# A sigmoid gate computed by its own table function, and another order of the last instructions of a decoder layer

## The chip, the cores and the metric

The kernel runs on one core of a Trainium2 chip. The metric is device time in microseconds (us), the median of several runs. The engines are named as the profile names them: PE (TensorE: matmuls; PEld are its weight loads), DVE (VectorE), ACT (ScalarE), POOL (GpSimd), SP (SyncE, which here only issues DMAs).

## The reference, cut to what matters

One layer of a decoder trunk on x of shape (1, 1024, 2048): an input projection feeds two groups of gated recurrences, their readouts go through an output projection, and then comes the stage that this change is about:

```python
h = h + y
e = rms_norm(p[i] @ ple_proj[i], ple_norm_w[i])
gate = jax.nn.sigmoid(rms_norm(h, ple_gate_norm_w[i]) @ ple_gate_w[i] + ple_gate_b[i])
h = h + (gate * e).astype(dtype)
return rms_norm(h, final_norm_w)
```

`ple_gate_w` is 2048 x 2048.

## The kernel before, in words

Everything is kept with features on the 128 partitions and tokens along the free dimension. There are 2048/128 = 16 feature tiles (KT) and two halves h of 512 tokens (TH). A product with a 2048 x 128 slab of weights is 16 steps of three fp32r matmuls 128x512 (weights and activations are split into a high and a low part; low times low is left out), so 48 matmuls a slab, collected in one PSUM bank `acc[par]`. The helper `passes` (L740 to L742) issues the three.

**The gate stage** is the last of the kernel: 32 slabs, 16 for each half. The semaphores `acc_free` and `acc_ready` hand the two PSUM banks back and forth, so PE may be a slab ahead of the elementwise work. For each tile c of half h:

- ACT `split_weights` casts the high part of the slab two ahead (2 x L1049), DVE `low_weights` makes the low part (2 x L1537); SP loads the raw weights.
- DVE `g_first`: g_t = acc * r_h (L2058, frees the PSUM bank), then g_t + bias (L2061).
- The sigmoid is exp(min(x,0) - ln(1 + exp(-|x|))): ACT `softplus` does Abs, Exp, Ln (L1055, L1057, L1059) into t1, DVE `log_sigmoid` the minimum and the subtraction (L1573) into t2, ACT `sigmoid` the last Exp (L1063).
- DVE `g_rest`: g_m = e * weight * r_e (L2070), times the sigmoid (L2075), plus the residual (L2077), times the final norm's weight (L2079), and the square's sum (L2083); ACT `g_gate` squares (L1438).

At the change from half 0 to half 1 ACT (`fill_high(5, k)`, L1107) and DVE (`fill_low`, L1556) also split the 16 activation tiles of the second half, eight before and eight after the gate of tile 14; the gate of tile 15 (`g_first(0, 7, 1)`) comes behind them on DVE. `row_rsqrt` (Ln, Exp) is called twice in the stage, for norm factors.

**The last slab** is done in two parts of 256 tokens, each a run of 48 matmuls 128x256, the first into `acc[1]`, the second into `ms_ps`, so that the end of the first part can overlap the second's matmuls. The functions with z_ in their names work on a part: DVE `z_product` (L2135), ACT `z_soft` (L1474, L1476, L1478), DVE `z_logs` (L2140), ACT `z_sigmoid` (L1483), DVE `z_gate` (L2146, L2148, L2150), ACT `z_square` (L1487). PE `row_products` (L1003, L1004) sums the squares over the features, DVE `z_variance` (L2155, L2157), ACT `z_rsqrt` (L1492, L1494) and DVE `z_factor` (a Newton step L1525 to L1531, then two diagonal matrices L2165, L2167) make the final norm's factors.

The 16 tiles of half 1 are then scaled and stored. The first six (N_TOK) go by tokens: PE `by_token` transposes them (L1014), ACT `z_token` scales them out of PSUM (L1501). The other ten go by features: PE `factors` (L1022) spreads the factors over the partitions, DVE `z_scale` multiplies (L2174). SP stores in a fixed order, for part 0 and then for part 1: two DMAs of the token tiles (L631, 512 and 256 KB) and five of the feature tiles (L635, 256 KB each), every one of them after the semaphore of its data. Each engine's order is written out by hand; nothing reorders it.

All of ACT's functions of the kernel before are in one function table, `natural_log_exp_and_others`, loaded once at the start (L1037).

Of the kernel before, what the change touches and what calls it, by code (L numbers as in the profile page):

```python
# [34 lines left out]
ALU = mybir.AluOpType  # L35
# [147 lines left out]
def build(nc, x_feat, p, slabs, w_glr, w2, vec, lb_rows, masks, restart, ident_d, out, e_scratch, y_scratch, w_sums, t_sums):  # L183
    with ExitStack() as ctx:
# [170 lines left out]
        g_arg = sem("g_arg")  # L355
# [34 lines left out]
        z_arg, z_sp, z_ls, z_sig = sem("z_arg"), sem("z_sp"), sem("z_ls"), sem("z_sig")  # L390
# [347 lines left out]
        def _(pe):  # L738
# [286 lines left out]
            row_products(0)  # L1025
            by_token(0)
            factors(0)
            row_products(1)
# [5 lines left out]
        def _(act):  # L1034
# [399 lines left out]
            def g_gate(h, c):  # L1434
                softplus(gate_sp(h, c), g_t, g_arg, c + (h * KT + 1))
                sigmoid(gate_sp(h, c))
                act.wait_ge(g2_sum, c + (h * KT + 1))
                A(t1, g_t, ACT.Square).then_inc(g2_sq, 1)  # L1438

            def g_pair(h, i):  # L1440
                for par in range(2):
                    g_split(h, i * 2 + par, par)
                    g_gate(h, i * 2 + par)

            g_pair(0, 0)
            st.fresh()
            g_pair(0, 1)
            row_rsqrt(ROWS_H[1], r_h[1], h_sum[1])
            st.fresh()
# [6 lines left out]
            g_gate(0, 14)  # L1456
# [4 lines left out]
            g_gate(0, 15)  # L1461
            g_pair(1, 0)
            row_rsqrt(ROWS_F[0], f_r[0], g_sum[0])
            st.fresh()
# [3 lines left out]
            g_gate(1, 14)  # L1468
            bias = gv_now[:, 1, 0:1]

            def z_soft(part):
                x = z_1[:, tokens(part)]
                act.wait_ge(z_arg, part + 1)
                st.mark(A(x, z_g[:, tokens(part)], ACT.Abs, bias=bias))  # L1474
                st.wait()
                st.mark(A(x, x, ACT.Exp, scale=-1.0))  # L1476
                st.wait()
                A(x, x, ACT.Ln, bias=1.0).then_inc(z_sp, 1)  # L1478

            def z_sigmoid(part):  # L1480
                x = z_2[:, tokens(part)]
                act.wait_ge(z_ls, part + 1)
                A(x, x, ACT.Exp, bias=bias).then_inc(z_sig, 1)  # L1483
# [19 lines left out]

            z_soft(0)
            z_sigmoid(0)
            z_square(0)
            z_soft(1)
            z_rsqrt(0)
            z_sigmoid(1)
            z_token(0, 0)  # L1510
            z_square(1)
            z_token(0, 1)
            z_rsqrt(1)
# [5 lines left out]
        def _(vec_e):  # L1519
# [532 lines left out]
            def g_first(h, i, par):  # L2052
# [4 lines left out]
                vec_e.wait_ge(acc_ready, tile_done(c + t_of(s_gate(h))) + OUT_SLABS)  # L2057
                v.tensor_tensor(g_t, acc[par][:, :], r_h[h], ALU.mult).then_inc(acc_free[par], 1)  # L2058
                vec_e.wait_ge(acc_free[par], tile_free(gate_pair(h, i)))
                st.wait()  # L2060
# [207 lines left out]
```

## Time and profile before

| | |
|---|---|
| median of 3 runs | 2192.04 us (2191.51 to 2192.65) |
| span of the profiled execution | 2189.4 us |
| PE busy | 2175.6 us, 99% of the span |
| DVE busy | 1520.5 us, 69% |
| ACT busy | 1014.7 us, 46% |
| POOL busy | 96.8 us, 4% |
| moved by DMA | 310.27 MB, mean 142 GB/s |

The span runs from the first to the last recorded instruction or transfer of one profiled execution; the median lies 2.6 us above it. A busy share says how long an engine had something to do, not that it sets the time. PE's two long times of doing nothing are in the last 19 us of the span, after the last slab's matmuls.

### The profile page before, as it was taken

The page shows a single profiled execution, that of the slowest core. Times are in us where ns is not written, and L with a number is a line of the kernel's source. Part 1 is how long each engine was busy: PE and PEld are TensorE (multiplying, and loading weights), DVE is VectorE, ACT ScalarE, POOL GpSimd, SP SyncE. Part 2 cuts the span into 40 slices and gives each one's busy share as a digit, 9 for nine tenths or more (in the row PEclk, how much of TensorE's full clock was granted, in tenths as well). Part 3 has the DMA queues.
Part 4 walks back from the last instruction along what each step waited for, and adds up shares of the span by engine and source line. Part 5 has one row for each costly group of instructions (what it writes and reads, how often), then busy time and mean ns, then how long its engine had stood idle before and what let it go on. Part 6 is the DMA issues. An engine that isn't in the chain of part 4 may idle for free.

```text
span 2189.4 us, 30587 instructions
## 1 busy us (share of the span) xinstructions
PE 2175.6 (99%) x10418; PEld 1821.7 (83%) x10418; DVE 1520.5 (69%) x3019; ACT 1014.7 (46%) x1759; POOL 96.8 (4%) x148
## 2 busy tenths in 40 slices
PE   9999999999999999999999999999999999999997
PEld 8888888888888888888888888888888888888886
DVE  7577777775666577766667565557667777768886
ACT  7454545444334354444445343335354445446554
POOL 1001011110000000000000000000110000000000
PEclk9999999999999999999999999999999999999998
DMA  9435665565432322232322545335576543332443
GB/s 338 170 102 163 171 178 168 165 177 145 125 99 86 97 69 87 85 126 81 115 99 93 173 152 141 98 108 145 187 250 235 173 163 115 121 123 98 159 161 127
DMA packets 100015, 310.27 MB, mean 142 GB/s; under 512 B 11360, under 2 KB 16736, under 8 KB 99168
## 3 DMA queue, kind: packets, MB, share of 16 engines
q1 hardware_dynamic: 88288, 248.42, 33.7%
q0 software_dynamic: 11648, 60.83, 10.9%
q8 instruction: 46, 0.75, 0.1%
q14 instruction: 33, 0.27, 0.0%
HBM read 284.04 MB, written 75.50 MB: 164 GB/s over the span
## 4 chain that ended last, share of the span: by engine, by line
PE 98%; DVE 1%; ACT 1%; issue 0%; DVEq 0%; ACTq 0%
PE acc L740 27%; PE acc L742 27%; PE acc L741 27%; PE lv L833 3%; PE so L842 1%; PE so L845 1%; PE so L822 1%; PE ms L742 1%; PE ms L741 1%; PE ms L740 1%; PE ms L811 1%; PE tr L741 1%; PE tr L742 1%; PE tr L740 1%; PE tr L857 0%; PE tr L807 0%
## 5 line engine op out<-in xcount | busy, mean ns | idle before, releaser
L740 PE MATMUL acc<-act_hi,w_lo 128*128 128x512 f32 (+1 forms) x2656 | 1063.0, 400 | 0.7 <-DVE work L2058 0.7
L742 PE MATMUL acc<-act_hi,w_hi 128*128 128x512 f32 (+1 forms) x2656 | 1033.9, 389 | 0.0
L741 PE MATMUL acc<-act_lo,w_hi 128*128 128x512 f32 (+1 forms) x2656 | 1033.4, 389 | 0.0
L742 PEld LDWEIGHTS acc<-act_hi,w_hi 128*128 128x128 f32 x2656 | 498.6, 188 | 104.9
L740 PEld LDWEIGHTS acc<-act_hi,w_lo 128*128 128x128 f32 x2656 | 499.7, 188 | 99.2 <-issue 3.9
L741 PEld LDWEIGHTS acc<-act_lo,w_hi 128*128 128x128 f32 x2656 | 500.0, 188 | 95.5 <-issue 1.7
L1049 ACT CAST w_hi<-w_raw 128x1024 fp32r<-128x1024 f32 x347 | 350.7, 1048 | 444.1 <-PE acc L742 357.5
L1537 DVE TENSOR_TENSOR w_lo<-w_raw,w_hi 128x1024 fp32r<-128x1024 f32 x347 | 410.7, 1220 | 104.4 <-ACT w_hi L1049 101.2
L1121 ACT ACTIVATE work<-work 128x512 f32<-128x512 f32 x120 | 75.7, 630 | 148.2 <-DVE work L1593 147.4
L1063 ACT ACTIVATE work<-work 128x512 f32<-128x512 f32 x95 | 60.1, 632 | 136.8 <-DVE work L1573 136.8
L1607 DVE COPY_PREDICATED work<-mask_sb,lv 128x256 f32<-128x256 uint8 x168 | 88.8, 529 | 7.3
L833 PEld LDWEIGHTS lv<-work 128*128 128x128 f32 x480 | 71.9, 190 | 9.4
L1599 DVE TENSOR_TENSOR work<-work 128x256 f32<-128x256 f32 x120 | 50.9, 424 | 39.4 <-ACT work L1121 39.3
L833 PE MATMUL lv<-work 128*128 128x128 f32 x480 | 72.6, 273 | 0.0
L1059 ACT ACTIVATE work<-work 128x512 f32<-128x512 f32 x103 | 65.2, 633 | 3.3
L1057 ACT ACTIVATE work<-work 128x512 f32<-128x512 f32 x103 | 65.2, 633 | 3.3
L1521 DVE MEMSET vec_dummy<- 128x1 f32 x230 | 13.6, 59 | 68.2 <-PE lv L833 63.5
L1578 DVE SCALAR_TENSOR_TENSOR work<-acc,work 128x512 f32<-128x512 f32 x48 | 33.2, 692 | 33.8 <-ACT work L1063 33.8
L1149 ACT ACTIVATE work<-work 128x128 f32<-128x128 f32 (+1 forms) x96 | 32.0, 334 | 41.5 <-DVE work L1642 41.5
L1593 DVE TENSOR_TENSOR work<-work 128x256 f32<-128x256 f32 x120 | 50.3, 419 | 0.0
L1592 DVE TENSOR_TENSOR work<-work 128x256 f32<-128x256 f32 x120 | 50.2, 419 | 0.0
L1600 DVE TENSOR_TENSOR work<-work 128x256 f32<-128x256 f32 x120 | 50.2, 418 | 0.0
(323 smaller groups left out, 2186.8 us busy)
## 6 DMA issues: line engine op xcount, KB each, us to landing
w_raw<-in_slabs SPq DMA_DIRECT2D x316, 512.0 KB, 4.5
w_sums<-in_slabs POOLq DMA_DIRECT2D x48, 512.0 KB, 6.3
w_raw<-w_sums SPq DMA_DIRECT2D x32, 512.0 KB, 4.2
work<-e_scratch SPq DMA_DIRECT2D x56, 256.0 KB, 2.8
t_sums<-y_scratch POOLq DMA_DIRECT2D x24, 512.0 KB, 6.8
feat<-in_x_feat SPq DMA_DIRECT2D x8, 1024.0 KB, 11.7
e_scratch<-work SPq DMA_DIRECT2D x32, 256.0 KB, 5.9
w_sums<-w_sums POOLq DMA_DIRECT2D x16, 512.0 KB, 3.9
```

What stands on the lines that cost most here:

```text
L740: nc.tensor.matmul(ps, lhs_lo, rhs_hi, start=start, stop=False)
L741: nc.tensor.matmul(ps, lhs_hi, rhs_lo, start=False, stop=False)
L742: return nc.tensor.matmul(ps, lhs_hi, rhs_hi, start=False, stop=stop)
L833: last = nc.tensor.matmul(scores[:, :, c * half:(c + 1) * half], x_lv[l % 3][:, c * C:(c + 1) * C], queries[:, :, c * half:(c + 1) * half] ...
L1049: nc.scalar.copy(w_hi[par][:, j, :], w_raw[j][:, :]).then_inc(w_hi_ready, 1)
L1057: st.mark(A(t1, t1, ACT.Exp, scale=-1.0))
L1059: A(t1, t1, ACT.Ln, bias=1.0).then_inc(sp_ready, 1)
L1063: A(t2, t2, ACT.Exp).then_inc(sig_ready, 1)
L1121: A(x_lv[l % 3], x_lv[l % 3], ACT.Exp).then_inc(lv_exp, 1)
L1537: v.tensor_tensor(w_lo[par][:, j, :], w_raw[j][:, :], w_hi[par][:, j, :].bitcast(F32), ALU.subtract).then_inc(w_lo_ready, 1)
L1599: st.mark(v.tensor_tensor(keys, keys, lower_tokens(k_t, s), ALU.mult))
L1607: v.copy_predicated(upper_tokens(attn, s), mask_sb[:, l, :].rearrange("p (b n s) -> p b n s", b=2, s=s), lv_ps[l % 2][:, 0:TH // 2].rearra ...
```

## The change

In the gate stage ACT computes one `Sigmoid` of g_t with the bias as its per-partition operand, in place of Abs, Exp, Ln and Exp; DVE's bias addition (L2061) and `log_sigmoid` (L1573) go. `Sigmoid` is in another function table than Ln and Exp, so `preload_act_table_set` calls are put in: to `sigmoid_and_others` at the start of the stage, to `natural_log_exp_and_others` and back around each of the two `row_rsqrt` of the stage, and to `natural_log_exp_and_others` behind the last two sigmoids. The gate's `act.wait_ge(acc_free...)` waits for DVE's product.

In the last slab `z_soft` and `z_logs` go, `z_sigmoid` is one Sigmoid of 128x256. ACT's order becomes sigmoid 0, sigmoid 1, table, square 0, square 1, rsqrt 0, rsqrt 1, tokens. DVE's becomes product 1, gate 0, gate 1, variance 0, factor 0, variance 1, factor 1, scale 0, scale 1. PE does row_products 0 and 1 ahead of the transposes. SP's order is unchanged.

```diff
@@ -352,7 +352,6 @@
         copied, summed = sem("copied"), sem("summed")
         t_copied, t_summed = sem("t_copied"), sem("t_summed")
         t_in_loaded = [sem(f"t_in_loaded{i}") for i in range(len(t_in))]
-        g_arg = sem("g_arg")
         acc_ready = sem("acc_ready")
         acc_free = [sem("acc_free0"), sem("acc_free1")]
         sp_ready, ls_ready, sig_ready = sem("sp_ready"), sem("ls_ready"), sem("sig_ready")
@@ -387,7 +386,7 @@
         tok_ready, tok_factor, tok_scaled = sem("tok_ready"), sem("tok_factor"), sem("tok_scaled")
         diag_ready, fbc_ready = sem("diag_ready"), sem("fbc_ready")
         cols_hi, cols_lo = sem("cols_hi"), sem("cols_lo")
-        z_arg, z_sp, z_ls, z_sig = sem("z_arg"), sem("z_sp"), sem("z_ls"), sem("z_sig")
+        z_arg, z_sig = sem("z_arg"), sem("z_sig")
         z_sum, z_sq, z_var, z_y0 = sem("z_sum"), sem("z_sq"), sem("z_var"), sem("z_y0")
         act_steps, vec_steps = sem("act_steps"), sem("vec_steps")
 
@@ -1023,9 +1022,9 @@
                 last.then_inc(fbc_ready, 1)
 
             row_products(0)
+            row_products(1)
             by_token(0)
             factors(0)
-            row_products(1)
             by_token(1)
             factors(1)
 
@@ -1431,21 +1430,24 @@
             def g_split(h, c, par):
                 split_weights(c + (s_gate(h) + 2), par, gate=True)
 
-            def g_gate(h, c):
-                softplus(gate_sp(h, c), g_t, g_arg, c + (h * KT + 1))
-                sigmoid(gate_sp(h, c))
+            def g_gate(h, c, par, i):
+                act.wait_ge(acc_free[par], tile_free(gate_pair(h, i)))
+                A(t2, g_t, ACT.Sigmoid, bias=gv_now[:, par, 0:1]).then_inc(sig_ready, 1)
                 act.wait_ge(g2_sum, c + (h * KT + 1))
                 A(t1, g_t, ACT.Square).then_inc(g2_sq, 1)
 
             def g_pair(h, i):
                 for par in range(2):
                     g_split(h, i * 2 + par, par)
-                    g_gate(h, i * 2 + par)
-
+                    g_gate(h, i * 2 + par, par, i)
+
+            act.preload_act_table_set("sigmoid_and_others")
             g_pair(0, 0)
             st.fresh()
             g_pair(0, 1)
+            act.preload_act_table_set("natural_log_exp_and_others")
             row_rsqrt(ROWS_H[1], r_h[1], h_sum[1])
+            act.preload_act_table_set("sigmoid_and_others")
             st.fresh()
             with act.Fori(2, KT // 2 - 1) as i:
                 g_pair(0, i)
@@ -1453,34 +1455,26 @@
             g_split(0, 14, 0)
             for k in range(HK):
                 fill_high(5, k)
-            g_gate(0, 14)
+            g_gate(0, 14, 0, 7)
             for k in range(HK, KT):
                 fill_high(5, k)
                 if k in (11, 14):
                     split_weights(s_gate(0) + 17, 1, (int(k == 14),))
-            g_gate(0, 15)
+            g_gate(0, 15, 1, 7)
             g_pair(1, 0)
+            act.preload_act_table_set("natural_log_exp_and_others")
             row_rsqrt(ROWS_F[0], f_r[0], g_sum[0])
+            act.preload_act_table_set("sigmoid_and_others")
             st.fresh()
             with act.Fori(1, KT // 2 - 1) as i:
                 g_pair(1, i)
                 st.fresh()
-            g_gate(1, 14)
+            g_gate(1, 14, 0, 7)
             bias = gv_now[:, 1, 0:1]
 
-            def z_soft(part):
-                x = z_1[:, tokens(part)]
+            def z_sigmoid(part):
                 act.wait_ge(z_arg, part + 1)
-                st.mark(A(x, z_g[:, tokens(part)], ACT.Abs, bias=bias))
-                st.wait()
-                st.mark(A(x, x, ACT.Exp, scale=-1.0))
-                st.wait()
-                A(x, x, ACT.Ln, bias=1.0).then_inc(z_sp, 1)
-
-            def z_sigmoid(part):
-                x = z_2[:, tokens(part)]
-                act.wait_ge(z_ls, part + 1)
-                A(x, x, ACT.Exp, bias=bias).then_inc(z_sig, 1)
+                A(z_2[:, tokens(part)], z_g[:, tokens(part)], ACT.Sigmoid, bias=bias).then_inc(z_sig, 1)
 
             def z_square(part):
                 act.wait_ge(z_sum, part + 1)
@@ -1501,16 +1495,15 @@
                     A(work[:, n0:n1, c * C:(c + 1) * C], tok_block(c)[u].rearrange("p (k n) -> p k n", n=C), ACT.Copy,
                       scale=f_tok[:, c:c + 1]).then_inc(tok_scaled, 1)
 
-            z_soft(0)
             z_sigmoid(0)
+            z_sigmoid(1)
+            act.preload_act_table_set("natural_log_exp_and_others")
             z_square(0)
-            z_soft(1)
+            z_square(1)
             z_rsqrt(0)
-            z_sigmoid(1)
+            z_rsqrt(1)
             z_token(0, 0)
-            z_square(1)
             z_token(0, 1)
-            z_rsqrt(1)
             z_token(1, 0)
             z_token(1, 1)
 
@@ -2055,10 +2048,8 @@
                 gv = gv_now[:, par, :]
                 st.mark(v.tensor_copy(gv[:, 0:3], g_vec[:, bass.ds(c * 3, 3)]))
                 vec_e.wait_ge(acc_ready, tile_done(c + t_of(s_gate(h))) + OUT_SLABS)
+                st.wait()
                 v.tensor_tensor(g_t, acc[par][:, :], r_h[h], ALU.mult).then_inc(acc_free[par], 1)
-                vec_e.wait_ge(acc_free[par], tile_free(gate_pair(h, i)))
-                st.wait()
-                v.tensor_scalar(g_t, g_t, gv[:, 0:1], None, ALU.add).then_inc(g_arg, 1)
 
             def g_rest(h, i, par, more_slabs=True, in_front_of_sum=None):
 
@@ -2070,7 +2061,6 @@
                 v.scalar_tensor_tensor(out=g_m, in0=e_in[par], scalar=gv[:, 1:2], in1=r_e[h],
                                        op0=ALU.mult, op1=ALU.mult).then_inc(e_used, 1)
                 vec_e.wait_ge(e_used, c + (h * KT + 1))
-                log_sigmoid(gate_sp(h, c), g_t)
                 vec_e.wait_ge(sig_ready, gate_sig(h, c) + 1)
                 st.mark(v.tensor_tensor(g_m, g_m, t2, ALU.mult))
                 st.wait()
@@ -2134,12 +2124,6 @@
                 vec_e.wait_ge(acc_ready, slab_done(SLABS - 1) + part)
                 v.tensor_tensor(z_g[:, tokens(part)], z_ps[part], r_h[1][:, tokens(part)], ALU.mult).then_inc(z_arg, 1)
 
-            def z_logs(part):
-                vec_e.wait_ge(z_sp, part + 1)
-                vec_e.wait_ge(z_arg, part + 1)
-                v.scalar_tensor_tensor(out=z_2[:, tokens(part)], in0=z_g[:, tokens(part)], scalar=gv[:, 3:4], in1=z_1[:, tokens(part)],
-                                       op0=ALU.min, op1=ALU.subtract).then_inc(z_ls, 1)
-
             def z_gate(part):
                 cols = tokens(part)
                 vec_e.wait_ge(z_sig, part + 1)
@@ -2176,22 +2160,17 @@
             g_first(1, 7, 0)
             st.mark(v.tensor_copy(gv[:, 0:3], g_vec[:, c * 3:c * 3 + 3]))
             st.wait()
-            st.mark(v.tensor_scalar(gv[:, 3:4], gv[:, 0:1], -1.0, None, ALU.mult))
             vec_e.wait_ge(e_loaded[1], KT * 16)
             st.mark(v.scalar_tensor_tensor(out=z_m, in0=e_in[1], scalar=gv[:, 1:2], in1=r_e[1], op0=ALU.mult, op1=ALU.mult))
             g_rest(1, 7, 0, False, in_front_of_sum=lambda: z_product(0))
-            z_logs(0)
+            z_product(1)
             z_gate(0)
-            z_product(1)
+            z_gate(1)
             z_variance(0)
-            z_logs(1)
             z_factor(0)
-            z_gate(1)
-            z_scale(0, N_TOK, N_TOK + 4)
             z_variance(1)
-            z_scale(0, N_TOK + 4, N_TOK + 6)
             z_factor(1)
-            z_scale(0, N_TOK + 6, KT)
+            z_scale(0, N_TOK, KT)
             z_scale(1, N_TOK, KT)
```

## Rows read from the trace of the kernel before

**Rows 1.** Waits of PE, the whole span: what it waited for, us in total, times, longest.

```profile
PE acc L740 <- DVE work L2058: 0.7, 1, 0.7
```

**Rows 2.** Timeline at the change of halves: start us, us, engine, line, operation, count [idle before].

```profile
1995.67 0.64 ACT L1438 ACTIVATE work<-work 128x512 f32<-128x512 f32 x1 [1.49 <-DVE work L2077]
...
2004.70 0.40 PE L742 MATMUL acc<-act_hi,w_hi 128*128 128x512 f32 x1
...
2005.02 0.68 DVE L2058 TENSOR_TENSOR work<-acc,glr_t 128x512 f32<-128x512 f32 x1
...
2005.76 0.50 PE L740 MATMUL acc<-act_hi,w_lo 128*128 128x512 f32 x1 [0.67 <-DVE work L2058]
...
2006.33 0.39 PE L742 MATMUL acc<-act_hi,w_hi 128*128 128x512 f32 x1
```

**Rows 3.** Groups by line, 1700 to 2170: count, busy us, mean ns, idle before.

```profile
L1057 ACT ACTIVATE work<-work 128x512 f32<-128x512 f32 x31 | 19.6, 633 | 1.0
...
L2075 DVE TENSOR_TENSOR work<-work 128x512 f32<-128x512 f32 x31 | 21.5, 693 | 21.6 <-ACT work L1063 21.6
...
L2061 DVE TENSOR_SCALAR work<-work,gv_now 128x512 f32<-128x512 f32 x31 | 15.1, 487 | 1.1
```

**Rows 4.** Windows of the gate stage: length, busy by engine (count), PEclk, DMA share, GB/s.

```profile
1860.00:1940.00 80.00, 80.00 (x353) 65.87 (x352) 57.65 (x90) 37.30 (x56) 0.00 (x0) 1.00 0.34 124
1940.00:2020.00 80.00, 79.33 (x349) 64.95 (x348) 62.36 (x93) 44.94 (x67) 0.00 (x0) 1.00 0.31 106
```

**Rows 5.** Timeline of the end, SP's first store.

```profile
2175.28 1.52 SPq L631 DMA_DIRECT2D out<-work  x2
```

**Rows 6.** Windows of the end: columns as in rows 4.

```profile
2176.00:2177.00 1.00, 1.00 (x11) 1.00 (x11) 1.00 (x4) 0.39 (x2) 0.00 (x0) 1.00 0.78 268
2177.00:2178.00 1.00, 1.00 (x9) 1.00 (x7) 0.97 (x6) 0.41 (x2) 0.00 (x0) 0.69 1.03 330
...
2188.00:2189.40 1.40, 0.00 (x0) 0.00 (x0) 0.00 (x0) 0.00 (x0) 0.00 (x0) 0.50 0.39 135
```

**Rows 7.** Timeline of the end, ACT.

```profile
2171.30 0.51 ACT L1474 ACTIVATE state_g<-glr_t,gv_now 128x256 f32<-128x256 f32 x1 [1.07 <-DVE glr_t L2135]
...
2173.99 1.27 ACT L1501 ACTIVATE work<-lv,small 128x512 f32<-128x512 f32 x2 [0.22 <-DVE small L1531]
2175.24 0.42 ACT L1487 ACTIVATE state_g<-glr_t 128x256 f32<-128x256 f32 x1
...
2177.65 0.20 ACT L1494 ACTIVATE small<-small 128x2 f32<-128x2 f32 x1
```

**Rows 8.** Timeline of the end, DVE.

```profile
2170.84 0.42 DVE L2135 TENSOR_TENSOR glr_t<-ms,state_h 128x256 f32<-128x256 f32 x1 [0.67 <-PE ms L742]
2171.63 0.16 DVE L2155 TENSOR_SCALAR small<-so 128x2 f32<-128x2 f32 x1 [0.36 <-PE so L1004]
...
2177.03 0.15 DVE L2155 TENSOR_SCALAR small<-ms 128x2 f32<-128x2 f32 x1
...
2179.15 1.41 DVE L2174 TENSOR_TENSOR work<-work,acc 128x256 f32<-128x256 f32 x4
```

**Rows 9.** Timeline of the end, PE.

```profile
2170.64 0.28 PE L1003 MATMUL so<-ones,state_g 128*128 128x1 f32 x2
...
2171.45 0.64 PE L1014 MATMUL lv<-ident,work 128*128 128x128 f32 x4
...
2172.58 0.38 PE L1014 MATMUL tr<-ident,work 128*128 128x128 f32 x2
...
2175.80 0.35 PE L1003 MATMUL ms<-ones,state_g 128*128 128x1 f32 x2 [0.62 <-ACT state_g L1487]
...
2177.38 1.04 PE L1014 MATMUL so<-ident,work 128*128 128x128 f32 x4
```

**Rows 10.** Timeline of the start, ACT: the one table load and what follows it.

```profile
0.75 1.28 ACT L1037 ACT_TABLE_LOAD   x1 [0.75 <-PEq L2256]
4.46 1.04 ACT L1049 CAST w_hi<-w_raw 128x1024 fp32r<-128x1024 f32 x1 [2.43 <-DMA w_raw<-in_slabs]
```

## The prediction, made before the changed kernel was run

> **What bounds the kernel now.** I read the busy times first: PE 99% of the span, ACT 46%, DVE 69%. So I asked for PE's waits. Up to the last slab there is one wait of PE on the stage that is changed, 0.7 us [rows 1]; in 80 us windows of the gate stage PE is busy 80.00 and 79.33 us [rows 4], the second being the window with that wait. So whatever ACT and DVE do between two slabs is hidden, except at that place. Two stretches are left in which less elementwise work can show: the change of halves, and what follows the last matmul.
>
> The change of halves [rows 2]. The last matmul of a slab starts at 2004.70, the next slab's first at 2005.76, because its PSUM bank is freed by L2058, which DVE reaches at 2005.02. The third matmul starts at 2006.33; at the pitch within a slab (80 us / 353 = 0.227 us, rows 4) it would have been 2004.70 + 3 x 0.227 = 2005.38. The stall costs 0.95 us.
>
> The end. PE's last slab matmul is over at about 2170.8: DVE takes its bank at 2170.84 [rows 8]. SP issues the first store of the second half at 2175.28 [rows 5]. From the window at 2176 the DMA share is 0.78, at 2177 it is 1.03, and I read all the 1 us windows up to 2188: each is at 0.99 or more, the last one (1.4 us) at 0.39 [rows 6]. The stores are 16 tiles of 128 x 512 x 4 bytes = 4.19 MB, at some 340 GB/s 12.3 us. So the end is bound by the transfers, which run without a gap from the first store on: the end comes 2189.4 - 2175.28 = 14.12 us after that issue, and whatever moves the first store moves the end. It is not bound by the last part's arithmetic, though the chain of work ends with it. The first store waits for ACT's two scaled token tiles (2173.99 + 1.27 = 2175.26) [rows 7].
>
> **The change part by part.**
>
> *Gate stage, 31 full tiles.* ACT loses three of four functions of 0.633 us, DVE loses L2061 (0.487) and L1573, about the size of L2075 (0.693) [rows 3]. On the chain of a tile the exchange with ACT of the last Exp goes too: L2075 waits 21.6 / 31 = 0.70 us for it. All is under PE's matmuls, cost or gain nil. Does a quieter ACT or DVE make matmuls faster? 80.00 us with 37.30 us of ACT hold 353 matmuls; 79.33 us with 44.94 us of ACT hold 349 [rows 4]: 0.2266 and 0.2273 with the stall's slow restart in the second, so no.
>
> *Table loads in the stage.* Five of 1.28 us each [rows 10]: one ahead of the first tile, four around the two row factors. ACT is idle for 80 - 37.3 = 42.7 of 80 us [rows 4], in pieces of some 3 us and more a slab, and weights are cast a slab ahead. Nil. If that cover were gone (loads put into every tile), two more a tile would be 2.6 us of some 5.8 idle per slab: still covered.
>
> *Change of halves.* ACT's second eight activation tiles start behind the square of tile 14 at 1995.67 [rows 2]. With L1573 (0.69) and the 0.70 us wait for Exp gone from that tile's chain, the sigmoid being ready long before, the square comes 1.39 us earlier. The fills, the weights and L2058 of tile 15 follow in order on ACT and DVE, so L2058 ends near 2005.70 - 1.39 = 2004.3, ahead of the 2004.93 at which PE wants the bank. Gain 0.95 us (bounds 0 and 0.95: later fills could wait for matmuls).
>
> *The end.* The new order puts work of the second part ahead of the first part's factors, on ACT, PE and DVE. Step by step to the first store:
> 1. Product 1 stays at 2170.84, sigmoid 1 on ACT from 2171.30, with bias, 0.51 us as L1474 [rows 7]: 2171.81.
> 2. Table load 1.28 [rows 10] with 0.03 to start: 2173.12. Nothing else covers it; the squares are queued behind it. DVE's gates of both parts, six operations of at most 0.46 us a step after 2171.26, have the sum of part 0 by 2172.2 and that of part 1 by 2173.5: not later than ACT needs them.
> 3. Square 0, 0.42, with a gap: 2173.57. PE starts row_products 0 0.14 later (2175.24 + 0.42 to 2175.80) [rows 7, 9]; variance 0 on DVE follows 0.99 after it (2170.64 to 2171.63) [rows 8, 9]: 2174.70.
> 4. ACT's rsqrt 1 now stands ahead of the tokens, and variance 1 stands behind factor 0 on DVE. From a variance to the end of its factor is 2179.15 - 2177.03 = 2.12 [rows 8]: variance 1 at 2176.82. Its rsqrt ends 2177.85 - 2177.03 = 0.82 later [rows 7, 8]: 2177.64.
> 5. Tokens 1.27, then the store: 2178.96. Against 2175.28 that is +3.68 us. In the kernel before rsqrt 0 had no load and no second part's squares ahead of it.
>
> PE's own line to the same point: from 2173.71 both row_products (0.81 each, 2170.64 to 2171.45) and twelve transposes (2171.45 to 2172.96, 1.51) [rows 9]: 2176.84, with 0.80 us to spare. That cover holds at the full clock. The granted clock is 1.00 at 2176, 0.69 in the next window and 0.50 at the end [rows 6], after little PE work; with the clock down four transposes take 1.04 instead of 0.64 us [rows 9]. In the new order PE has nothing from 2170.8 to 2173.7, where it had the row products and transposes, so the fall may come earlier. Bounds: no cost, if it falls after 2176.04; if all 3.13 us of PE's line double, it ends at 2179.97, 2.3 us after ACT is ready. For a fall evenly placed between 2173.7 and 2177.4 the mean is 2.33 x 2.33 / 2 / 3.7 = 0.7 us. I take 0.7. The Trainium skill, "TensorE: Matmul & The Clock Gate", section "What's actually happening", says that the throttled clock is the default and activity releases it; by that the fall comes early and the cost is at the 2.3 us end.
>
> After the first store the supply is enough: 512 KB are 1.5 us of transfer, the second token pair comes 0.8 us later, and each 256 KB of feature tiles takes DVE two multiplies of 0.35 [rows 8], 0.71 us, for 0.77 us of transfer. Part 1's multiplies follow without a gap.
>
> Sum: +3.68 + 0.7 - 0.95 = +3.4 us. The span would be 2189.4 + 3.4 = 2192.8; the median lies 2.6 us above the span, so 2192.04 + 3.4 = 2195.5 us, 0.16% more.
>
> **The rivals.**
>
> *Slower: ACT loses more at the table switch before the squares, and PE is cold.* The trace shows the load at 0.75 for 1.28 us and the next ACT work at 4.46, released by a DMA [rows 10], so up to 2.43 us behind a load would be unseen. Half of that, 1.2 us, in step 2 moves the store to 3.68 + 1.2 = 4.9, and PE's line starts at 2174.9, so that the clock costs some 1.4 on average: +5.4 in all after the 0.95, 2197.4 us. It decides (slower by over 0.2%) once load's tail and clock together cost over 1.7 us. For it: nothing covers ACT between 2171.8 and 2173.6. Against: the profile gives the load as one instruction with nothing behind. The Trainium skill, "ScalarE: Activation LUTs", section "What ACT_TABLE_LOAD costs", gives 1283 ns, which agrees with the row, and a drain of 1380 ns beside it, which no run here shows; with it my sum would be an estimated 1.4 us and its share of the clock higher. Chance 0.25.
>
> *The end is not bound by the transfers but by DVE's last multiply.* For it: the chain ends on DVE; the DMA share is a share of engines, and could rise in rate with tiles ready in advance. Then before's last multiply, 2179.15 + 14 x 0.35 = 2184.1, is compared with scale 0 starting at 2177.64 + 1.30 (factor 1, 2177.85 to 2179.15) = 2178.94 and 20 x 0.353: 2186.0. +1.9 - 0.95 = +1.0, 2193.0 us. Against: twelve windows at 0.99 or more. Chance 0.1.
>
> *Faster: matmuls speed up with ACT and DVE quieter.* To come out 4.4 us under before, 7.8 us are to be won from the 32 x 48 = 1536 matmuls, 5 ns of 227 each: 2187.6 us. Rows 4 speak against it. Chance 0.03.
>
> *The change does not do what it says* (loads in every loop pass, the stall at the change of halves stays): hidden on ACT as shown; the stall kept gives 2196.4. It is within the forecast's own range.
>
> **How the numbers follow.** The forecast has 0.62, its own range 2194.5 (clock and stall at their best, 3.68 - 0.95 = +2.7, a little less for gaps) to 2197.1 (all cold, 3.68 + 2.33 - 0.95). The range for 8 in 10 takes in half of the DVE case below and the load's tail above: 2193.4 to 2198.4. What a measurement of this kernel can tell from no change is about 0.2%, 4.4 us: slower means above 2196.4, faster below 2187.7. Slower: a sixth of the forecast (clock falls in its first 0.7 us), 0.1, and most of the first rival, 0.2, together 0.3. Faster: 0.03. Within: 0.67.
>
> **What would show it.** One table load each near 1833, two near 1865 and 2020, one at 2171.8; PE's wait on L2058 gone; the pitch still 0.227; a Sigmoid of 0.6 to 0.7 us for 128x512; square 0 at 2173.1, variance 0 at 2174.7, the first L1501 at 2177.7 and the first store near 2179.0 to 2179.7 (all less 0.95 if the stall is gone); 14.1 us from it to the end at a full DMA share. I am wrong if the switch costs more than its record, if the clock falls at once after the last slab, if the transfers leave gaps or go faster, or if PE waits at a new place in the gate stage.

## The result

| | before | changed |
|---|---|---|
| median of 20 runs | 2192.59 us (2190.99 to 2195.72) | 2196.70 us (2195.28 to 2198.06) |
| span of the profiled execution | 2189.4 us | 2196.1 us |
| ACT busy | 1014.7 us | 963.1 us |
| DVE busy | 1520.5 us | 1486.4 us |

The ratio is 1.0018, with a 95% interval of 1.0012 to 1.0024: the kernel is 4.1 us slower by the medians, although ACT and DVE have 52 and 34 us less to do. The forecast was +3.4 us.

The profiled executions differ by 6.7 us, more than the medians. Of that, 1.6 us lie in code that the change does not touch: a step of the first half's norm (ACT, `r_e<-sq_sum`) starts at 541.30 us where it started at 539.69. A kernel of the experiments that has the old gate stage shows the same shift (below), so it belongs to an execution and not to the change. The profiled execution of the changed kernel is also the slowest of its 20 (2198.06 us). To be free of such shifts I read the end of every trace from one event, the start of DVE's product for part 1 (`z_product(1)`, here called P), which follows the last matmul of the last slab.

**Gate stage.** The waits of PE in the changed kernel, whole span (columns as in [rows 1]):

```profile
PE so L1002 <- ACT state_g L1481: 2.9, 1, 2.9
PE tr L927 <- DVE ones L1855: 1.6, 1, 1.6
PE tr L856 <- DVE work L1647: 0.5, 1, 0.5
PE lv L832 <- DVE x_lv L1593: 0.2, 1, 0.2
```

The wait for the PSUM bank at the change of halves [rows 1, 2] is gone; the 1.6 us stand before as well, the two small ones below them are in the recurrences, far ahead of the gate stage, and the 2.9 us are new and at the end. The groups by line, 1700 to 2170 us, and the window that had the stall:

```profile
L1435 ACT ACTIVATE work<-work,gv_now 128x512 f32<-128x512 f32 x31 | 22.3, 720 | 9.0 <-DVE work L2052 9.0
L2065 DVE TENSOR_TENSOR work<-work 128x512 f32<-128x512 f32 x31 | 21.5, 693 | 3.0
```

```profile
1940.00:2020.00 80.00, 80.00 (x353) 65.87 (x352) 55.86 (x80) 32.92 (x46) 0.00 (x0) 1.00 0.30 106
```

One Sigmoid with its bias takes 0.720 us in place of four functions of 0.63; the multiplication by it (L2065) waits 3.0 us in all where L2075 waited 21.6 [rows 3]. PE now has 353 matmuls in that window, as in its neighbour, where it had 349 [rows 4]. The pitch did not change. Around the row factors ACT has the extra loads and is still in time for the next weights:

```profile
1871.59 1.28 ACT L1448 ACT_TABLE_LOAD   x1
1873.06 0.60 ACT L1066 ACTIVATE state_g<-lv 128x512 f32<-128x512 f32 x1 [0.19 <-DVE lv L1536]
1873.69 0.63 ACT L1068 ACTIVATE state_h<-state_g 128x512 f32<-128x512 f32 x1
1874.35 1.28 ACT L1450 ACT_TABLE_LOAD   x1
1875.64 0.19 ACT L1034 COPY act_dummy<-vecs 128x1 f32<-128x1 f32 x1
1876.30 2.00 ACT L1048 CAST w_hi<-w_raw 128x1024 fp32r<-128x1024 f32 x2 [0.47 <-PE acc L741]
```

The cast at 1876.30 waits for PE's previous slab, not for the load.

**The end.** ACT of the changed kernel (timeline, columns as in [rows 2]), the counterpart of [rows 7]:

```profile
2172.04 0.51 ACT L1477 ACTIVATE r_e<-glr_t,gv_now 128x256 f32<-128x256 f32 x1 [5.32 <-DVE glr_t L2125]
2172.56 1.28 ACT L1500 ACT_TABLE_LOAD   x1
2173.86 0.72 ACT L1481 ACTIVATE state_g<-glr_t 128x256 f32<-128x256 f32 x2
...
2178.96 0.20 ACT L1488 ACTIVATE small<-small 128x2 f32<-128x2 f32 x1
2180.67 1.27 ACT L1495 ACTIVATE work<-lv,small 128x512 f32<-128x512 f32 x2 [1.50 <-PE tr L1013]
```

PE, the counterpart of [rows 9], and SP's first store, of [rows 5]:

```profile
2174.42 0.56 PE L1002 MATMUL so<-ones,state_g 128*128 128x1 f32 x2 [2.95 <-ACT state_g L1481]
...
2177.40 0.56 PE L1003 MATMUL ms<-ones,state_g 128*128 128x1 f32 x2
2177.83 1.09 PE L1013 MATMUL lv<-ident,work 128*128 128x128 f32 x4
...
2179.99 0.64 PE L1013 MATMUL tr<-ident,work 128*128 128x128 f32 x2
```

```profile
2181.96 1.12 SPq L630 DMA_DIRECT2D out<-work  x2
```

P is at 2171.58. The squares follow the load by 0.02 us. ACT's own chain is through at 2179.16, and then it waits 1.50 us for PE's transposes, which PE does at 0.21 us each instead of 0.11 [rows 9]. The granted clock (windows of 1 us, columns as in [rows 4]):

```profile
2172.00:2173.00 1.00, 0.00 (x0) 0.00 (x0) 0.93 (x4) 0.94 (x2) 0.00 (x0) 1.00 0.00 0
2173.00:2174.00 1.00, 0.00 (x0) 0.00 (x0) 0.94 (x3) 0.99 (x2) 0.00 (x0) 0.81 0.00 0
2174.00:2175.00 1.00, 0.58 (x3) 0.61 (x4) 0.35 (x1) 0.58 (x2) 0.00 (x0) 0.50 0.00 0
```

It is down to one half (1.2 of 2.4 GHz) before PE's first row product, after more than 2 us in which PE had nothing. The first store is at P + 10.38 us, where before had P + 4.44 (2175.28 - 2170.84). From the store to the end it is 2196.1 - 2181.96 = 14.14 us, where it was 14.12. So P to the end went from 18.56 to 24.52 us, +5.96, and 5.94 of it lie ahead of the first store.

### The profile page after: what moved, and what is told of

It reads as the page before. It is cut to its first block, busy times and chain, and to the rows that moved or that the text cites. A ratio compares the mean times of both kernels' runs of the same rounds, so it can differ in the third digit from the quotient of the medians.

```text
span 2196.1 us, 30330 instructions
## 1 busy us (share of the span) xinstructions
PE 2179.0 (99%) x10418; PEld 1825.2 (83%) x10418; DVE 1486.4 (68%) x2954; ACT 963.1 (44%) x1666; POOL 96.6 (4%) x148
## 4 chain that ended last, share of the span: by engine, by line
PE 94%; DMA 2%; DVE 2%; ACT 1%; issue 1%; DVEq 0%; SPq 0%; ACTq 0%
PE acc L739 26%; PE acc L741 26%; PE acc L740 26%; PE lv L832 3%; DMA w_raw<-in_slabs 2%; PE so L841 1%; PE so L844 1%; PE so L821 1%; PE ms L739 1%; PE ms L740 1%; PE ms L741 1%; PE tr L739 1%; PE tr L740 1%; PE tr L741 1%; PE ms L810 1%
## 5 line engine op out<-in xcount | busy, mean ns | idle before, releaser
L1120 ACT ACTIVATE work<-work 128x512 f32<-128x512 f32 x120 | 75.8, 632 | 150.1 <-DVE work L1586 149.4
L1062 ACT ACTIVATE work<-work 128x512 f32<-128x512 f32 x64 | 40.5, 633 | 95.6 <-DVE work L1566 95.6
L1437 ACT ACTIVATE work<-work 128x512 f32<-128x512 f32 x31 | 19.7, 636 | 96.2 <-DVE work L2067 96.2
L1571 DVE SCALAR_TENSOR_TENSOR work<-acc,work 128x512 f32<-128x512 f32 x48 | 33.2, 692 | 33.9 <-ACT work L1062 33.9
L1566 DVE SCALAR_TENSOR_TENSOR work<-acc,work 128x512 f32<-128x512 f32 x64 | 44.0, 688 | 8.8 <-ACT work L1058 3.7
```

The source lines that it names most:

```text
L1120: A(x_lv[l % 3], x_lv[l % 3], ACT.Exp).then_inc(lv_exp, 1)
```

## The experiments

All times after P are from one profiled execution of each kernel, and they are the sharper measure: the runs of one kernel spread by 1 to 5 us, while "rest" stays within 0.1 us in ten of the fourteen kernels and "store" differed by 1.0 us between two executions of the changed one. "Store" is the first store after P, "rest" the time from it to the end of the span. The ratio is taken as recorded; it differs from the quotient of the two medians by up to 0.0003.

| kernel | P | store | rest | median, before beside it | ratio (95%) |
|---|---|---|---|---|---|
| before | 2170.84 | 4.44 | 14.12 | | |
| changed | 2171.58 | 10.38 | 14.14 | 2196.70, 2192.59 | 1.0018 (1.0012 to 1.0024) |
| changed again | 2170.37 | 9.40 | 14.13 | 2195.82 (one run) | |
| gate stage only | 2169.50 | 4.44 | 14.16 | 2190.79, 2192.10 | 0.9997 (0.9988 to 1.0006) |
| end only | 2172.43 | 10.37 | 14.10 | 2197.21, 2192.10 | 1.0025 (1.0014 to 1.0036) |
| 24 matmuls in the gap | 2169.89 | 10.12 | 14.09 | 2196.34, 2192.10 | 1.0019 (1.0010 to 1.0028) |
| 12 matmuls in the gap | 2169.73 | 7.95 | 14.12 | 2194.75, 2191.74 | 1.0012 (1.0002 to 1.0021) |
| load behind squares | 2170.18 | 7.81 | 14.11 | 2194.43, 2192.10 | 1.0011 (1.0002 to 1.0021) |
| transposes first | 2170.65 | 7.95 | 14.10 | 2194.80, 2192.36 | 1.0011 (1.0002 to 1.0021) |
| no load, new order | 2171.25 | 9.27 | 14.08 | 2195.74, 2192.36 | 1.0012 (1.0003 to 1.0021) |
| no load, old order | 2169.72 | 3.79 | 14.39 | 2190.30, 2192.36 | 0.9994 (0.9985 to 1.0003) |
| load, old order | 2170.80 | 4.89 | 14.41 | 2191.52, 2191.74 | 0.9999 (0.9990 to 1.0008) |
| early rsqrt | 2171.53 | 3.80 | 15.47 | 2192.69, 2192.36 | 0.9999 (0.9990 to 1.0008) |
| early rsqrt, scale sooner | 2169.45 | 3.79 | 17.06 | 2193.09, 2191.74 | 1.0006 (0.9997 to 1.0016) |

### Each half of the change by itself

Gate stage only: the last slab's functions and order of before, and the load back ahead of it (the diff is against the changed kernel).

```diff
             g_gate(1, 14, 0, 7)
+            act.preload_act_table_set("natural_log_exp_and_others")
             bias = gv_now[:, 1, 0:1]
...
-            z_sigmoid(0)
-            z_sigmoid(1)
+            z_soft(0)
+            z_sigmoid(0)
+            z_square(0)
+            z_soft(1)
...
```

> The changed gate stage with its table loads, but the last slab as before (Abs, Exp, Ln, minimum, Exp, the old order); one more table load ahead of the last slab's first part, under matmuls. My theory: the stage is worth -0.95 us (the stall at the change of halves), the end costs nothing: ratio to before 0.9996, some 2191.6, and in its trace the first store 4.44 us after the second product as before. Rival (the table loads cost in the stage, or the changed kernel's 1.6 us loss before 540 us belongs to the change): ratio 1.000 to 1.0003, and the second product at about 2170.8 or later.

Measured: 0.9997, store and rest as in before. PE has no wait for a PSUM bank any more. The ratio's interval holds 1, so the times don't show the 0.95 us; the traces do. P at 2169.50 is 1.3 us earlier than before's, but it varies by 2 us among the twelve executions with the new gate stage (2169.45 to 2171.58, mean 2170.39), so that number alone would prove nothing. The variation lies ahead of the stage: the norm's step of the first half starts anywhere from 539.24 to 541.33 us. From that step to P it is 1631.15 us in before and 1631.25 in the other kernel with the old gate stage (next), and 1630.17 to 1630.32 in eleven of the twelve with the new one (1630.72 in the twelfth, which has two waits of 0.2 us on PE's way). So the gate stage gives 0.83 to 1.08 us, as worked out.

End only: before's gate stage, a load ahead of `z_sigmoid(0)`, then the changed end (the diff is against before).

```diff
+            act.preload_act_table_set("sigmoid_and_others")
             bias = gv_now[:, 1, 0:1]
...
+            z_sigmoid(0)
+            z_sigmoid(1)
+            act.preload_act_table_set("natural_log_exp_and_others")
+            z_square(0)
...
```

> The gate stage as before, the last slab as in the change (one Sigmoid a part, a table load ahead of the part-0 sigmoid under matmuls, one behind the sigmoids, the new order). My theory: it carries the whole loss and more: the first store 10.4 us after the second product where before has 4.44, so +5 to +6 us, ratio 1.0023 to 1.0027. Rival (the loss is spread over the stage, or is the transfers'): less than +4 us, ratio under 1.0018.

Measured: 1.0025, store at 10.37. The whole loss is in the end, and the gate stage pays a little of it back. This kernel has before's gate stage and P at 2172.43: the 1.6 us by which executions differ ahead of the end are none of the change's. Its wait at the change of halves is there again:

```profile
PE acc L740 <- DVE work L2048: 0.7, 1, 0.7
```

### Is it the clock?

```diff
+            pe.wait_ge(g2_ready, KT + N_TOK)
+            for _ in range(24):
+                nc.tensor.matmul(lv_ps[0][:, 0:P], ones[:, :], ones[:, :], start=True, stop=True)
             row_products(0)
             row_products(1)
```

> The changed kernel with 24 matmuls of ones 128x128 on PE between the last slab and the row products, where PE had 2.9 us of nothing. My theory of the clock: the granted clock stays 1.00 over the row products and transposes, PE's line falls from 6.25 to 3.1 us and ACT's own chain is late next: the first store 8.1 us after the second product instead of 10.4, so about -2.3 us against the changed kernel. Rival (PE's clock costs nothing there, ACT's chain sets the store): no change, 10.4 us.

The store came at 10.12, which looks like the rival's 10.4. The trace says why:

```profile
2169.62 5.52 PE L1026 MATMUL lv<-ones 128*128 128x128 f32 x48
2174.97 0.28 PE L1002 MATMUL so<-ones,state_g 128*128 128x1 f32 x2
```

I had mis-sized the filling: each fp32 matmul counts as two of 0.11 us, so 24 took 5.4 us, and the row products began 5.08 us after P instead of 2.84. But from the first row product to the first scaled tokens it now took 2178.74 - 2174.97 = 3.77 us, where the changed kernel took 6.25. So the same with 12:

```diff
-            for _ in range(24):
+            for _ in range(12):
```

> As the kernel with 24 matmuls of ones in PE's gap, with 12: the 24 took 5.4 us and pushed the row products from 2.84 to 5.08 us after the second product. Twelve take 2.7 us and should end just as the squares do. If the clock was what made PE's line 6.25 us: the clock stays at 1.00, the first tokens are scaled 6.8 us and the first store issued 8.1 us after the second product (10.4 in the changed kernel), ratio to before 1.0009 to 1.0014. If not: 10.4.

```profile
2172.57 0.35 PE L1002 MATMUL so<-ones,state_g 128*128 128x1 f32 x2 [0.27 <-ACT state_g L1484]
...
2175.47 0.38 PE L1013 MATMUL tr<-ident,work 128*128 128x128 f32 x2
```

The store is at 7.95, 2.4 us earlier than in the changed kernel, with nothing removed and matmuls added that compute nothing of use. The granted clock stays at 1.00 up to 2180.7, PE's line of row products and transposes is 3.28 us long (2172.57 to 2175.85), and ACT is late next. This shows the clock's share of that execution of the changed kernel: 2.4 us of the 5.9. The medians say less: 4.1 us above before for the changed kernel and 3.0 for this one, 1.1 us apart, with intervals that overlap.

> The changed kernel once more, to see where the granted clock falls and how far the first store is from the second product in another execution. If the fall depends on what PE did: at about 2 us after the product again and 10.4 us. If it moves from run to run: anything from 8.1 to 10.4 us.

In another execution of the changed kernel the same row products run half at the full clock:

```profile
2173.21 0.35 PE L1002 MATMUL so<-ones,state_g 128*128 128x1 f32 x2 [2.95 <-ACT state_g L1481]
...
2174.09 0.40 PE L1002 MATMUL ms<-ones,state_g 128*128 128x1 f32 x2
2174.36 0.57 PE L1003 MATMUL ms<-ones,state_g 128*128 128x1 f32 x2
```

The fall comes about 3.9 us after P here and about 2.0 after P in the first, the work being the same; the store is at 9.40. "End only" has the same tail once more: there the fall comes 2.7 us after P, just ahead of the first row product, and the store is at 10.37. So the place of the fall moves from execution to execution, and with it the clock's share: 1.4 us here (9.40 - 7.95), 2.4 in the two others.

### Is it the order on PE?

```diff
+            by_token(0)
             row_products(0)
             row_products(1)
-            by_token(0)
```

> The changed kernel with PE's first twelve transposes ahead of the two row_products, so in the gap in which PE waits for the squares. My theory (PE's line of row products and transposes at half clock sets the first store): the store is 8.2 to 9.0 us after the second product instead of 10.4, and the clock falls later or the same. Rival (ACT's load and the two rsqrts in a row set it, clock without effect): 10.4 stays, or 8.1 at least only by the clock.

7.95 us, a little better than the 8.2 expected. The transposes filled the gap, the row products still ran at full clock, and PE has only the row products left between the squares and the factors:

```profile
2173.49 0.35 PE L1002 MATMUL so<-ones,state_g 128*128 128x1 f32 x2 [1.64 <-ACT state_g L1481]
...
2177.33 1.25 ACT L1495 ACTIVATE work<-lv,small 128x512 f32<-128x512 f32 x2
```

So both ways of making PE punctual end at the same 7.95 us, which is ACT's and DVE's chain.

### Is it the load?

Load behind the squares:

```diff
-            act.preload_act_table_set("natural_log_exp_and_others")
             z_square(0)
             z_square(1)
+            act.preload_act_table_set("natural_log_exp_and_others")
             z_rsqrt(0)
```

> The changed kernel with the last table load behind the two squares instead of ahead of them. Both squares can start 1.6 and 0.4 us earlier, the load then runs beside PE's row products. If PE's line at half clock sets the first store: it starts 1.04 us earlier and the store is at 9.3 us after the second product, -1.0 us against the changed kernel. If ACT's chain set it (load 1.28 us on it in either place): no gain, 10.4 us.

7.81, better than either number. The row products started 1.80 us after P and still at full clock, the clock fell only in the transposes (4.7 us after P), and rsqrt 0 waited for the load. So this kernel doesn't separate the load from the clock. Nor did the earlier start save the clock, as the next kernel shows.

No load at all, new order. Ln and Exp of the last norm's factors are replaced by copies, so this kernel leaves out the inverse root and its second half of the output is scaled wrongly; the instructions are otherwise the same.

```diff
-            act.preload_act_table_set("natural_log_exp_and_others")
...
-                st.mark(A(f_tmp[:, cols], f_var[:, cols], ACT.Ln))
+                st.mark(A(f_tmp[:, cols], f_var[:, cols], ACT.Copy))
...
-                A(f_tok[:, cols], f_tmp[:, cols], ACT.Exp, scale=-0.5).then_inc(z_y0, 1)
+                A(f_tok[:, cols], f_tmp[:, cols], ACT.Copy, scale=-0.5).then_inc(z_y0, 1)
```

> The changed kernel without the last table load: the Ln and Exp of the last norm's factors are replaced by copies (so the output's second half is scaled wrongly; same instructions otherwise), squares straight behind the sigmoids. Measures what the load costs beside the kernel with the load behind the squares (first store 7.8 us after the second product, rsqrt 0 waiting 1.1 us for the load). If only the load stood in the way: 6.7 us. If PE's transposes are late next: 7.2 us. Against the changed kernel (10.4) that is 3.2 to 3.7 us less, ratio to before 1.0004 to 1.0007; what is left over before's 4.4 us is then the order alone.

This missed: 9.27, not 6.7 to 7.2. The clock fell about 2 us after P, as in the first execution of the changed kernel, so PE's line was at half clock from its start:

```profile
2173.07 0.48 PE L1002 MATMUL so<-ones,state_g 128*128 128x1 f32 x2 [1.92 <-ACT state_g L1481]
...
2179.23 1.26 ACT L1495 ACTIVATE work<-lv,small 128x512 f32<-128x512 f32 x2 [1.50 <-PE tr L1013]
```

The load's absence brings PE's line forward by 1.0 us (from P + 2.84 to P + 1.82), and the store by 1.1 (10.38 to 9.27). The kernels without load and with the load behind the squares have the same start of PE's line (1.82 and 1.80 us after P) after the same idle time of PE (1.92 us), but the clock fell 1.9 us after P in the one and 4.7 in the other. For that the one without load is 1.5 us later, although it has less to do.

Old order, no load, and old order with it, on all three engines (the diff shows ACT's side of the first; its Ln and Exp are copies again, and in the second they are kept and the load stands between sigmoid 1 and rsqrt 0):

```diff
             z_sigmoid(0)
+            z_square(0)
             z_sigmoid(1)
-            z_square(0)
-            z_square(1)
             z_rsqrt(0)
-            z_rsqrt(1)
             z_token(0, 0)
+            z_square(1)
...
```

> The changed gate stage and one Sigmoid a part in the last slab, but the order of before on PE, ACT and DVE and no table load (Ln and Exp of the last factors replaced by copies, so the output's second half is scaled wrongly). My theory: the order is most of the loss; with the old one the first store comes 3.8 us after the second product, 0.6 earlier than in before because rsqrt 0 needn't wait for the part-1 Abs, Exp, Ln; ratio to before 0.9993. Rival (the order costs nothing, the load everything): the store at the same distance as in the kernel without load in the new order, 6.7 us or more.

> The change in the order of before: the changed gate stage, one Sigmoid a part in the last slab, the table load between sigmoid 1 and rsqrt 0 and nothing else moved. The load then costs what it delays rsqrt 0: it ends 2.3 us after the second product where rsqrt 0 could start at 1.2, so the first store at 4.9 us (4.4 before, 3.8 without load, 10.4 in the change); with the stage's 0.95 us the kernel is 0.5 to 0 us faster than before, ratio 0.9997 to 1.0000. Rival (the load is the main cause of the change's loss): store beyond 6 us, ratio over 1.0005.

3.79 and 4.89, both as expected to 0.01 us. With the order of before the load costs 1.10 us of the store, and Sigmoid without it would gain 0.65 over before's 4.44. In both the rest is 14.4 us, 0.3 longer than elsewhere, with no gap in the transfers (in the kernel with the load the DMA share is at 0.96 or more in every 1 us window from 2177 to 2189); no run shows why. With the load the kernel can't be told from before (0.9999). The timeline of ACT with the load and of DVE's part-0 variance:

```profile
2171.78 1.28 ACT L1501 ACT_TABLE_LOAD   x1
...
2174.40 1.27 ACT L1495 ACTIVATE work<-lv,small 128x512 f32<-128x512 f32 x2 [0.88 <-DVE small L1524]
```

```profile
2171.59 0.16 DVE L2139 TENSOR_SCALAR small<-so 128x2 f32<-128x2 f32 x1 [0.36 <-PE so L1003]
```

The variance starts 0.79 us after P, as in before, since PE sums part 0's squares straight behind the last matmul; in the changed kernel it starts 4.72 after P (2176.30).

### Does the first store set the end?

With the changed gate stage and Abs, Exp, Ln kept in the last slab, ACT's rsqrt 0 was put between the part-1 Abs and Exp, and DVE's factor 0 ahead of the part-1 minimum. ACT's first tokens moved too, the four-tile group ahead of the part-1 sigmoid and the other ahead of square 1, which makes part 1 later (the diff is against before, cut):

```diff
                 st.mark(A(x, z_g[:, tokens(part)], ACT.Abs, bias=bias))
+                if part:
+                    z_rsqrt(0)
                 st.wait()
...
             z_soft(1)
-            z_rsqrt(0)
-            z_sigmoid(1)
             z_token(0, 0)
-            z_square(1)
+            z_sigmoid(1)
             z_token(0, 1)
+            z_square(1)
...
-            z_logs(1)
             z_factor(0)
+            z_logs(1)
```

> The changed gate stage, the last slab as before with Abs, Exp, Ln, but rsqrt 0 put between the part-1 Abs and Exp, factor 0 ahead of the part-1 minimum, and the first tokens ahead of the part-1 last Exp. If the first store sets the end: the store comes 3.8 us after the second product (4.4 before), the end 0.6 us earlier than with the old tail, 14.1 us behind the store: ratio to before 0.9993, some 2190.5. If the end is set by the second part's work: that is up to 1.4 us later, and the end gains nothing, ratio 0.9997.

The store came at 3.80, but 15.47 us passed from it to the end. Windows of the end of this kernel:

```profile
2178.00:2179.00 1.00, 1.00 (x10) 1.00 (x10) 0.97 (x5) 0.18 (x1) 0.00 (x0) 0.81 0.77 266
2179.00:2180.00 1.00, 1.00 (x7) 1.00 (x5) 0.90 (x6) 0.22 (x2) 0.00 (x0) 0.50 1.04 343
2180.00:2181.00 1.00, 0.72 (x3) 0.32 (x3) 0.96 (x5) 0.55 (x1) 0.00 (x0) 0.50 0.97 318
2181.00:2182.00 1.00, 0.92 (x4) 0.62 (x3) 1.00 (x4) 1.00 (x4) 0.00 (x0) 0.50 0.18 58
```

The DMA share drops to 0.18, because SP has no tile ready for it. Its third store of part 0's feature tiles is issued at 2179.48, the fourth 1.84 us later. The fourth waits for the first two of DVE's last four multiplications of part 0, which are queued behind part 1's variance and factor:

```profile
2180.36 0.28 DVE L2170 TENSOR_SCALAR work<-ident,small 128x128 f32<-128x128 f32 x1
2180.55 1.41 DVE L2177 TENSOR_TENSOR work<-work,acc 128x256 f32<-128x256 f32 x4
...
2181.32 0.37 SPq L634 DMA_DIRECT2D out<-work  x1
```

A smaller gap (0.77 at 2178) lies behind the tokens, since the first feature tile is stored only at 2177.89. Before has the same 1.84 us between its third and fourth store (2178.08 and 2179.92), but they come 0.71 us earlier after P and the transfers still queued cover them. I then moved four multiplications of part 0 ahead of the part-1 gate:

```diff
             z_logs(1)
-            z_gate(1)
             z_scale(0, N_TOK, N_TOK + 4)
+            z_gate(1)
```

> As the kernel with the early rsqrt, but DVE multiplies the first four feature tiles of part 0 ahead of the part-1 gate. There the store came at 3.8 us, yet 15.5 us passed from it to the end instead of 14.1, which I read as a gap in the transfers: the first feature tile was stored only 2.6 us after the first tokens. If so: that gap closes here, but the second part comes 0.8 us later, so 14.1 to 14.9 us from the first store to the end. Rival (the end hangs on the second part's work, whatever the first stores do): 15.5 us or more.

It got worse, 17.06: the early gap closed and the later one grew. Part 1's row products start 6.53 us after P (5.68 in the kernel above) and at half clock, and DVE's last six multiplications of part 0 stand behind the variance that waits for them:

```profile
2178.00:2179.00 1.00, 1.00 (x7) 1.00 (x6) 0.93 (x6) 0.41 (x2) 0.00 (x0) 0.50 0.03 9
2179.00:2180.00 1.00, 1.00 (x6) 1.00 (x6) 0.90 (x6) 0.00 (x0) 0.00 (x0) 0.50 0.18 61
```

So my 14.1 us behind the first store is a floor, and it holds as long as every later tile is ready in time; part 0's own last tiles, which wait behind part 1's factor, are the first that are not. Before is close to that edge. None of the kernels is measurably faster than before; the gate stage alone (0.9997) is the best of those that compute everything.

## Why the prediction was right, and where it was mis-sized

- **The stage is hidden under PE.** Right: five loads, 31 Sigmoids and shorter chains changed nothing but the one stall; the pitch stayed at 353 matmuls in 80 us.
- **The stall at the change of halves goes, 0.95 us.** Right by the traces (0.83 to 1.08 from the norm's step to P); by the times it is below what they resolve.
- **The end hangs on the first store, by 14.12 us.** Right for this change (14.14, and 14.08 to 14.16 in eight more executions), but I took it for a rule of the stage, "whatever moves the first store moves the end". It is one only as long as the later tiles are ready in time: 15.47 and 17.06 where they were not. In the two kernels with Sigmoid in the old order it is 14.4, for one of them with a store 0.45 us later than before's, and that is not explained. (The full windows behind the first store are eleven, 2177 to 2187, not twelve.)
- **The chain to the store, +3.68 us.** Predicted distances after P: square 0 at 2.31, variance 0 at 3.86, rsqrt 1 through at 6.80, store at 8.12. With the clock held up by twelve matmuls: square 0 at 2.28, variance at 3.90, rsqrt 1 through at 6.76, store at 7.95, so +3.51. The steps were right, 0.17 us apart from what was worked out.
- **The clock, 0.7 us.** The mechanism was right, the term was mis-sized. It is the mean over falls placed evenly between 2173.7 and 2177.4, that is 2.9 to 6.6 us after P, which let PE do part of its line at full clock in every case. In the three executions with this tail the fall came 2.0, 2.7 and 3.9 us after P, the first two ahead of that range, and cost 2.4, 2.4 and 1.4 us. The bound of 2.3 us at the all-cold end was met: 2.4.
- **Sum.** -0.95 + 3.51 + 1.4 to 2.4 = +4.0 to +5.0 us; the medians differ by 4.1, which would leave an estimated 1.5 us for the clock. The forecast's +3.4 was below by the clock's term. Of the 1.2 us between 2195.5 and 2196.70, 0.55 are before's own median, 2192.04 in three runs and 2192.59 in twenty. That the kernel came out within 0.2% of before was close: 4.1 of 4.4 us, and the ratio's interval reaches beyond it.
- **The slower rival.** It joined two mechanisms. The hidden cost behind a load is not there: the squares start 0.02 us behind it, at 2173.86. By the Trainium skill, "ScalarE: Activation LUTs", section "What ACT_TABLE_LOAD costs", 1380 ns of drain were to follow; no run here shows them. The other half, a cold PE, is what happened.
- **The DVE-bound and the faster rival** did not occur: DVE's last multiplications were through well before the transfers, and PE's pitch did not move.
- **What the load and the order cost.** The prediction named both and did not part them. The store's +5.94 us are -0.65 for Sigmoid in place of the chain of functions (4.44 to 3.79), +1.10 for the load (to 4.89), +3.06 for the new order with the clock up (to 7.95) and +2.43 for the clock in the profiled execution (to 10.38). The order, which the load suggested (it puts both sigmoids ahead and both squares behind), is the largest part: it makes part 0 wait for part 1 on three engines. It also moves PE's work behind a gap of 2.9 us, and there the clock falls before or during that work.

What stays open: why an execution is up to 2.1 us later by 541 us than another in unchanged code (539.24 to 541.33 us), which was seen in kernels with either gate stage; what places the fall of the clock, which differs by 2.8 us (1.9 and 4.7 us after P) between two kernels with the same idle time of PE; and the 0.3 us behind the first store in the old order with Sigmoid. That filled gaps keep the clock up rests on three executions (24 matmuls, 12 matmuls, transposes first), in which it fell 5.75 us after P at the earliest, against 1.9 to 4.7 in the five with the gap.

## What to carry to other kernels

Where one engine is busy 99% of the span, a change that takes 50 us of work from the others is worth the stalls it removes, here one of 0.95 us, and it is decided by the few microseconds after that engine's last instruction. There, count from the last matmul to the first store, ask of each engine what is now queued ahead of the first part, and don't group operations for the sake of one table load if that makes the first part wait for the second. A gap that opens on PE ahead of small matmuls can cost twice, once for itself and once for the clock behind it (here 1.4 to 2.4 us): put independent PE work, such as transposes, into the gap.

## What the runs showed of the hardware that I had not expected

- Twelve fp32 matmuls of ones in an otherwise idle stretch of PE brought the first store forward by 2.4 us against one execution of the same kernel without them and by 1.4 against another. Row products 128x1 are affected as much as transposes: pairs follow each other at 0.22 us at a granted clock of 1.00 and at 0.43 us at 0.50, though they stream a single column.
- In the same work the fall of the clock came about 2 us after P in one execution and 3.9 us in another, and the first store differs by 1 us with it (10.38 and 9.40).
- A table load held ACT for 1.28 us and no longer; the instruction behind it started 0.02 us later (2172.56 + 1.28 = 2173.84, and 2173.86).
